# Moving the down products of a feed-forward pair one slot later, behind the first quarter of the next up chunk

## What is computed

```python
h = x @ w_in                       # columns q | k | v | u, 512 each
a_out = stick_breaking(q, k, v)    # 8 heads of 64, strictly causal
p_out = pool_mix(u)                # trailing means over 2, 4, 8, 16 tokens
x1 = LayerNorm(ALPHA * x + concat[a_out, p_out] @ w_out)
ffn = (silu(x1 @ w_gate) * (x1 @ w_up)) @ w_down        # hidden width 2816
y = LayerNorm(ALPHA * x1 + ffn)
```

## Time and profile before

| | before |
|---|---|
| median of three runs | 2588.72 us |
| span of the profiled execution, first to last instruction | 2585.7 us |
| PE busy | 2521.1 us, 98% of the span |
| VectorE busy | 1574.1 us, 61% |
| ScalarE busy | 1154.3 us, 45% |
| GpSimd busy | 1172.3 us, 45% |
| DMA | 374.43 MB, mean 145 GB/s |

### The profile page before, as it was taken

One profiled execution on the slowest core, in us unless ns is written; L12 is line 12 of the kernel. 1 busy time (PEld: TensorE's weight loads), 2 busy tenths in 40 slices (PEclk: granted clock), 3 DMA queues, 4 the chain that ended last, 5 costly groups with the idle time before them and its releaser, 6 DMA issues.

```text
span 2585.7 us, 37584 instructions
## 1 busy us (share of the span) xinstructions
PE 2521.1 (98%) x13894; PEld 2147.9 (83%) x13894; DVE 1574.1 (61%) x2125; ACT 1154.3 (45%) x1932; POOL 1172.3 (45%) x1028
## 2 busy tenths in 40 slices
PE   9999999999999999999999999999999999999998
PEld 9978798787878888878788877878878897999997
DVE  3266336666444357787744477787775345867676
ACT  4465326665232135566531265656654213343333
POOL 4465437755223135456631174556653213354434
PEclk9999999999999999999999999999999999999999
DMA  7697956764446243444254244333532612333232
GB/s 231 193 281 249 355 169 194 225 216 125 136 134 236 82 115 106 127 118 112 89 207 139 98 117 124 103 110 103 147 103 96 223 60 90 96 98 114 91 94 88
DMA packets 211158, 374.43 MB, mean 145 GB/s; under 512 B 30784, under 2 KB 105152, under 8 KB 208928
## 3 DMA queue, kind: packets, MB, share of 16 engines
q1 hardware_dynamic: 210976, 372.02, 45.7%
HBM read 303.86 MB, written 68.09 MB: 144 GB/s over the span
## 4 chain that ended last, share of the span: by engine, by line
PE 82%; DVE 7%; issue 4%; ACT 3%; POOL 2%; DMA 2%; SPq 1%; DVEq 0%; POOLq 0%; ACTq 0%
PE bank L1290 26%; PE bank L1352 19%; PE bank L1240 8%; PE bank L1194 7%; PE bank L1298 7%; PE bank L1092 5%; PE bank L1139 4%; PE bank L1108 4%; DVE left L1922 1%; DMA gw_lo_raw<-in_w_in_dram 1%; DVE acc L1960 1%; POOL gw_lo L2592 1%; PE bank L1217 1%; ACT beta L1476 1%; DVE stats L1942 0%
## 5 line engine op out<-in xcount | busy, mean ns | idle before, releaser
L1290 PE MATMUL bank<-x1T,gw_hi 128*128 128x512 f32 (+1 forms) x2336 | 712.2, 388 | 3.7 <-DVE hT_lo_raw L2036 2.3
L2522 POOL TENSOR_TENSOR beta<-beta,left 128x512 f32<-128x512 f32 (+2 forms) x326 | 352.5, 1082 | 349.7 <-DVE left L1922 349.2
L1290 PEld LDWEIGHTS bank<-x1T,gw_hi 128*128 128x128 f32 x2336 | 418.8, 188 | 83.7 <-issue 3.2
L1290 PE MATMUL bank<-x1T,gw_lo 128*128 128x512 f32 (+1 forms) x1168 | 447.9, 383 | 0.0
L2549 POOL TENSOR_TENSOR gw_lo<-gw_lo_raw,gw_hi 128x1024 fp32r<-128x1024 f32 x70 | 181.7, 2596 | 424.1 <-ACT gw_hi L1544 423.9
L1467 ACT ACTIVATE aT<-bank 128x512 fp32r<-128x512 f32 (+2 forms) x326 | 173.6, 533 | 427.4 <-PE bank L1108 376.0
L1240 PE MATMUL bank<-x1T,gw_hi 128*128 128x256 f32 (+2 forms) x1472 | 354.6, 333 | 6.3 <-DVE gw_lo L2231 2.5
L2217 DVE TENSOR_TENSOR acc<-bank,acc 128x512 f32<-128x512 f32 x312 | 213.3, 686 | 214.1 <-PE bank L1352 210.6
L1907 DVE TENSOR_TENSOR aT<-bank,aT 128x512 fp32r<-128x512 f32 (+2 forms) x326 | 196.9, 604 | 197.6 <-ACT aT L1467 196.3
L1352 PE MATMUL bank<-dw_hi,hT_hi 128*128 128x512 f32 x728 | 295.6, 406 | 9.8 <-issue 5.7
L1352 PE MATMUL bank<-dw_lo,hT_hi 128*128 128x512 f32 x728 | 287.0, 394 | 0.0
(11 more groups left out here) (223 smaller groups left out, 4709.3 us busy)
## 6 DMA issues: line engine op xcount, KB each, us to landing
gw_lo_raw<-in_w_gate_dram SPq DMA_DIRECT2D x88, 512.0 KB, 3.7
gw_lo_raw<-in_w_up_dram SPq DMA_DIRECT2D x88, 512.0 KB, 3.8
dw_lo_raw<-in_w_down_dram SPq DMA_DIRECT2D x86, 512.0 KB, 4.4
gw_lo_raw<-in_w_in_dram SPq DMA_DIRECT2D x64, 512.0 KB, 4.5
k_st<-kT_scratch SPq DMA_DIRECT2D x160, 128.0 KB, 4.1
v_st<-v_scratch SPq DMA_DIRECT2D x80, 256.0 KB, 4.2
q_st<-qT_scratch SPq DMA_DIRECT2D x128, 128.0 KB, 3.9
wo_raw<-in_w_out_dram SPq DMA_DIRECT2D x16, 1024.0 KB, 5.7
```

Of the source, the lines that this page charges most:

```text
L1290: m = pe.matmul(gu_bank(g, n)[:, 0:w], gw[L % 4][a][:, k, :], x1T[x][:, k, first:first + w], start=k == 0 and s == 0, stop=k == KD - 1 and ...
L2522: pool.tensor_tensor(x[:, 0:w], x[:, 0:w], left[n % RL][:, 1:w + 1], ALU.mult).then_inc(a_done, 1)
```

## The change

On every engine the block of eight slots that holds the down products of the pair before is moved behind the first slot of the up product of chunk 0. The slots of a pair are then: 0 to 3 gate of chunk 0, 4 the first quarter of up of chunk 0, 5 to 12 the down products, 13 to 15 the other three quarters of up, and 16 to 23 as before. The table `due` is not changed, so the attention and MIX steps keep their slot numbers. `sigmoid` of chunk 0 goes from slot 12 to slot 13, `times_gate` of chunk 0 from slot 13 to slot 14, and the load of the next `w_down` chunks from ahead of slot 12 to ahead of slot 13. In the first pair of blocks 1 to 3, where no down products stand, `sigmoid`, `times_gate` and the load move one slot later too. All else keeps its slot, among it the statistics and centring of the second layer norm in group 1, i = 2 (slot 14), which stand ahead of `times_gate` in the source.

```diff
+    STORE_PAIR, WINO_SHIFT, DOWNS_FROM = 4, 3, 1
...
@@ TensorE
-                    if p:
-                        for d in range(2 * tiles_of(b)):
-                            if not is_last(b, p):
-                                downs(b, p - 1, d)
-                            background(next(slot))
                     for e, g in ((0, 1), (1, 0), (1, 1)) if b + p else ((1, 0), (1, 1)):
                         for i in range(4):
+                            if (e, g, i) == (0, 1, DOWNS_FROM) and p:
+                                for d in range(2 * tiles_of(b)):
+                                    downs(b, p - 1, d)
+                                    background(next(slot))
                             gate(b, p, e, g, i)
                             background(next(slot))
...
@@ ScalarE
                     for i in range(4):
+                        if i == DOWNS_FROM and p:
+                            for d in range(2 * tiles_of(b)):
+                                background(next(slot))
+                                if before_wino and d in (2, 3, 4):
+                                    tokens_hi((3, 2, 4)[d - 2])
                         background(next(slot))
-                        if i == (0 if pair else 2):
+                        if i == (DOWNS_FROM if pair else 2):
                             sigmoid(b, p, 0)
...
@@ VectorE
                     for i in range(4):
+                        if i == DOWNS_FROM and p:
+                            for d in range(2 * tiles_of(b)):
+                                add_down(b, p - 1, d)
+                                background(next(slot))
...
                         now = ahead(next(slot))
                         second_norm(b, p, 1, i)
-                        if i == (1 if pair else 3):
+                        if i == (DOWNS_FROM + 1 if pair else 3):
                             times_gate(b, p, 0)
                         behind(now)
                         if i == 2 and before_wino:
                             tokens_lo(4, 2)
-                        if i != 1 and before_wino:
-                            quarter_sums(0, ((S_1, None, S_2, S_4)[i],))
+                        if i and before_wino:
+                            quarter_sums(0, ((None, S_1, S_2, S_4)[i],))
...
@@ SyncE (GpSimd's loop is moved in the same way)
-                    if p:
-                        for d in range(2 * tiles_of(b)):
-                            background(next(slot))
                     for i in range(4):
-                        if i == 0:
+                        if i == DOWNS_FROM and p:
+                            for d in range(2 * tiles_of(b)):
+                                background(next(slot))
+                        if i == DOWNS_FROM:
                             load_down(b, p)
                         background(next(slot))
```

More of the change, by code:

```diff
@@ L664, in stream @@
     SHIFT_AT = [(3, 0, 2), (3, 1, 0), (3, 2, 0), (4, 0, 2)]
-    STORE_PAIR, WINO_SHIFT = 4, 3
+    STORE_PAIR, WINO_SHIFT, DOWNS_FROM = 4, 3, 1
     with nc.Block() as block:
@@ L1812, in _ @@
                         second_norm(b, p, 0, i)
[L1813 to L1817, removed]
-                    for i in range(4):
+                    for i in range(4):
+                        if i == DOWNS_FROM and p:
[3 more added lines that the diff above has]
+                                    tokens_hi((3, 2, 4)[d - 2])
                         background(next(slot))
-                        if i == (0 if pair else 2):
+                        if i == (DOWNS_FROM if pair else 2):
                             sigmoid(b, p, 0)
@@ L2393, in _ @@
                         second_norm(b, p, 0, i)
[L2394 to L2402, removed]
-                    for i in range(4):
+                    for i in range(4):
+                        if i == DOWNS_FROM and p:
+                            for d in range(2 * tiles_of(b)):
+                                add_down(b, p - 1, d)
+                                background(next(slot))
+                                if before_wino and d in (0, 5, 8):
+                                    if d == 0:
+                                        token_sum(7)
+                                    else:
+                                        tokens_lo((3, 2)[d // 8], d // 8)
                         now = ahead(next(slot))
                         second_norm(b, p, 1, i)
-                        if i == (1 if pair else 3):
+                        if i == (DOWNS_FROM + 1 if pair else 3):
                             times_gate(b, p, 0)
```

## The result

| | before | changed |
|---|---|---|
| median | 2588.91 us (21 runs) | 2593.58 us (21 runs) |
| ratio, 95% interval | | 1.0018, 1.0013 to 1.0024 |
| span of the profiled execution | 2585.7 us | 2593.4 us |

The change costs 4.7 us by the medians (6.5 us were forecast), which is 0.18%, and 7.7 us between the two profiled executions. The two differ because of which executions were profiled. In the changed kernel's, the time (2595.22 us) is 1.8 us more than the span and 1.6 us above the median. So the 3.0 us that stood between span and median of before are not all outside the span.

What follows compares the result with a forecast made beforehand. The prediction took PE, busy 98% of the span, as the bound. Losses of 12.4 us plus 3.4 us of slow clock minus gains of 9.3 us made 6.5 us, so 2595.2 us; likeliest range 2593 to 2598, 8-in-10 range 2589.5 to 2600.

Steps and rivals of the forecast that it cites:

- gain at `hidden_lo`: PE's short waits ahead of the down products vanish with a slot more slack; 4.8 us gained.
- gain at `add_down`, pair 1.4: PE's wait at the down products for a late VectorE vanishes; 0.9 us gained with the overlap.
- pair 0.9, wait and clock: PE's wait for `add_down` goes, 1.9 us, and the slow clock behind it, 1.7 us.
- (a): Attention in slots 13 and 14 delays `times_gate` in pairs 1.2, 0.10, 1.9 and 2.5; 4.0 us lost.
- (b): Layer norm ahead of `times_gate` makes it late in pairs 2.0, 1.0, 1.1, 0.8 and 1.8; 5.8 us lost.
- (c): Chains from the later last down product, pairs 3.1 and 2.10, plus a subtraction in 2.8; 2.6 us lost.
- (d): Longer idle stretches in pair 2.10 and at 3.2 each bring slow clock, 1.7 us apiece; 3.4 us lost.
- Rival 2: A third of the 9.8 us `times_gate` losses returns in later waits, one clock drop comes; 2590.2 us, chance 0.13.
- Rival 1: The clock stays up or falls once more at most, rest as forecast; 2591.8 up to 2593.5 us, chance 0.24.
- Rival 3: `times_gate` is not late, so its losses and the clock drops fall away; 2582.0 us, chance 0.06.
- Rival 4: New waits for `summed` like pair 0.9's arise, each up to 1.9 + 1.7 us; 2600 us, chance 0.15.
- signs named ahead: PE's waits: "issue" under 2 us, `times_gate` about 11, six pairs over 1 each, line 1298 3.5, up weights about 3.

Runs made afterwards that it cites:

- e1: Changed kernel with sigmoid and `times_gate` of chunk 0 back where they stood before, so only the down products are later; 2587.06 us, 0.9997 of before.
- e2: Kernel before with only sigmoid and `times_gate` of chunk 0 one slot later, down products not moved; 2595.29 us, 1.0028 of before.
- e5: As e1, but with pairs 0.8, 1.8, 2.9, 2.10 and 3.1 entirely in the order of before; 2581.30 us, 0.9972 of before.
- e6: Changed kernel with `times_gate` of chunk 0 first in slot 14, ahead of that slot's attention and layer norm; 2586.35 us, 0.9990 of before.
- e8: Kernel before with only `hidden_lo` of chunk 1 moved ahead of VectorE's attention step of slot 2; 2582.93 us, 0.9981 of before.
- e4: Changed kernel with the edits of e1 and e3 together; 2587.49 us, 0.9997 of before.
- e9: e8 with down products one slot later in pairs 0.9 and 1.4 only, `times_gate` first in its slot there; 2580.66 us, 0.9968 of before.
- e10: e7 with e8's edit, `hidden_lo` of chunk 1 ahead of the attention step of slot 2; 2578.35 us, 0.9956 of before.
- e7: e6 with pairs 0.8, 1.8, 2.10 and 3.1 entirely in the order of before; 2582.01 us, 0.9973 of before.
- e3: Changed kernel with the old order in pairs 2.10 and 3.1 only; 2589.99 us, 1.0004 of before.
- e11: Changed kernel with GpSimd's two down-weight casts of pair 3.1 held back until VectorE's last cast for pair 3.2; 2592.52 us, 1.0017 of before.

## Why the prediction came out right

**The direction and most terms.** Forecast was a loss of 6.5 us; the ledger says 6.3, the medians 4.7. The time of 2593.58 us lies 1.6 us under the likeliest 2595.2 and in its range. The outcome by class was not the one that had the largest chance: +0.18% is "within 0.2%" (0.39), not "slower by over 0.2%" (0.55).

| step | forecast | ledger |
|---|---|---|
| gain at `hidden_lo` (0.1, 1.3, 1.10, 2.2, 2.5, 2.6) | -4.8 | -4.8 |
| gain at `add_down`, pair 1.4 | -0.9 | -1.07 |
| pair 0.9, wait and clock | -3.6 | -2.66 |
| (a) 1.2, 0.10, 1.9, 2.5 | +4.0 | +3.3 |
| (b) 2.0, 1.0, 1.1, 0.8, 1.8 | +5.8 | +5.8 |
| (c) 3.1 to 3.2, 2.10, 2.8 | +2.6 | +2.8 |
| (d) two stretches at 1.2 GHz | +3.4 | +2.4 |
| near 2543 us, not forecast | 0 | +0.6 |

(Pair 2.5's -0.73 is split by e1 and e2 into a gain of 0.9 and a loss of 0.2. How the clock is split off stands under "Sizes".) That the two sums agree to 0.2 us is in part luck: the losses (a) and (d) were taken 0.7 and 1.0 us too large, which the gain of pair 0.9, taken 0.9 too large, and the 0.6 us not foreseen nearly make up for.

**`times_gate` is the loss, the down products the gain.** e1 and e2 do the two halves of the change apart: -1.6 us and +6.7 us by the medians, together near the +4.7 of both. By the runs alone e1 is no faster than before (0.9988 to 1.0006); the gain of the later down products is seen in its ledger, where the six waits for `hidden_lo` and the two for `add_down` bring 8.6 us (1.6 of them the slow clock of pair 0.9), and in e5, which takes the losing pairs out and is 7.2 us faster. e6 shows that what makes `times_gate` late is what stands ahead of it in slot 14, as (a) and (b) had it, except in pairs 0.8 and 1.8.

**Waits for `hidden_lo`.** That PE waits because `hidden_lo` stands behind an attention step is shown by e8, which cures the waits by that order alone. The part of pair 2.6 that I took back (0.7) is right too: the changed kernel waits 0.80 us for the scan there, and e8, without that wait, gains 1.35 against 0.61.

**Sizes that were off.** In pair 0.9 I took the wait of 1.79 us for gained entirely. The changed kernel's timeline shows why it isn't:

```profile
968.71 0.41 PE L1108 MATMUL bank<-begin,beta 128*128 128x128 f32 x2 [0.47 <-POOL beta L2521]
```

PE, no longer held up by `add_down`, comes to its transposes before GpSimd's `beta` is there. In pair 1.9 the wait came (0.90 us idle), but PE's 0.36 us of "issue" five slots behind vanished with it, so 0.55 us stays of 1.2. In pair 0.8 the eighth down product waits 1.64 us and `times_gate` another 0.85, 2.4 us for my 1.8. In pair 2.8 `times_gate` stands behind both subtractions of line 1975, 6.68 us together where the second had taken 3.90 us before, 1.27 us for my 0.4. At pair 3.2 I carried the chain over as it was, 1.5 us longer. It got 0.8 longer, since one of VectorE's subtractions in it (`xt_lo`, line 2104 before, 2103 now) fell nearer to the end of the GpSimd cast beside it and took 2.80 us for 3.48 (below).

The slow clock (d) cost less than 1.7 us a stretch. In pair 2.10, e6 has the changed kernel's wait (2.80 us) and no slow stretch, and loses 0.76 us against 2.29, so the stretch cost 1.5 us. At pair 3.2 it cost up to 1.5 us by the 20th matmul behind the wait, but only 0.8 to 0.9 us from the 40th on, in each of the seven kernels that had it there (the changed one, e1, e4, e6, e8, e9, e10). Before, PE had waited another 0.42 us there for VectorE's `xt_lo`; a slower PE comes later and doesn't wait. The 0.6 us near 2543 us are a wait for VectorE (line 2113), with 1.2 us in e5, 0.6 in e4 and nothing in e7. Its cause is open.

**Rival 2, partly given back,** is refuted for the feed-forward pairs by e2's ledger: five losses of 0.55 to 1.38 us, and no pair behind them gains more than 0.03 us (0.9 apart, told above). Only the wait ahead of pair 3.2 is 0.7 us shorter there, 1.29 us, with `times_gate` in another place of VectorE's chain. The 3.0 us between the profiles' 7.7 and the medians' 4.7 are no time given back either. In the profiled executions the changed kernel had two more stretches at 1.2 GHz than the kernel before from 560 us on, 3.4 us. Averaged over the runs the clocks differ by 0.0008 (0.9973 in 31 runs of before, 0.9965), 2.1 us. That is 1.3 of the 3.0 us; the rest I can't place, and it is within what the stage ahead of pair 0.1 moves from one execution to the next (-1.5 to +3.4 us against before in these profiles).

**Rival 1, the clock,** did not come in the profiled execution, where the clock fell behind both waits. Behind the same two waits it stayed up in other kernels, so it was right to give it a chance: see below. **Rival 3** is refuted: PE waits 0.85 to 1.44 us for `times_gate` in every pair of (a) and (b) but 1.1 and 2.5, which had been put at 0.5 and 0.2 us. **Rival 4** did not come: the waits for `add_down` sum up to 3.3 us for 3.1 before, and the two long ones (1.64 us in pair 0.8, 1.24 in pair 2.10) stand where (b) and (c) had put something. Of the signs named ahead, "issue" (0.8 us), the waits for `times_gate` (9.8 for 11) and the up weights (2.8 for 3) came as said. Pairs 0.8 and 1.9 stayed under 1 us (0.85 and 0.90), and line 1298 waited 2.8 us for 3.5.

## What to carry to other kernels

When a consumer waits for a producer that stands behind other work on its engine, move the producer ahead of that work first: two lines on one engine (e8) brought 5.5 us and cost nothing elsewhere. A slot's shift of the down products on five engines cost 4.7 us, and brought 7.2 us only when the pairs were picked (e5). A slot of slack given to one dependency is taken from the others in the same ring, and before moving a block one lists the deadlines behind it, pair by pair, since the pairs that gain (idle ahead of the block) and those that lose (no slack behind it) are different ones and can be ordered differently. A ledger of the critical engine's progress between fixed marks tells what a wait is finally worth; sums of waits don't.

## What the runs showed of the hardware that I had not expected

**The length of an idle stretch of PE alone doesn't tell whether the clock falls.** In the feed-forward part of the 14 profiles PE had 71 idle stretches of over 1.2 us. A stretch at 1.2 GHz began in or behind 6 of the 46 under 1.7 us, 8 of the 15 up to 2.1 us, and 8 of the 10 longer ones. The place counts as well: all 6 of the short ones are the same wait in pair 0.4, near 757 us, where the clock fell in 6 of 8 cases, and it fell behind none of the 38 other stretches under 1.7 us. What sets that place apart isn't shown. The same stretch of 2.0 us ahead of pair 3.2 was followed by it in four kernels (e4, e8, e9, e10) and not in four others (before, e3, e5, e7), and 2.80 us in pair 2.10 went without it in e1 and e6. The wait in e1, and the window behind it:

```profile
2159.47 0.50 PE L1290 MATMUL bank<-x1T,gw_hi 128*128 128x512 f32 x1 [2.80 <-POOL gw_lo L2550]
```

```profile
2159.47:2162.88 3.41, 3.41 (x15) 2.77 (x16) 0.00 (x0) 0.00 (x0) 3.41 (x2) 1.00 0.02 8
```

Each time it lasted 3.41 us or twice that, and cost 0.8 to 1.6 us per 3.41 where the ledger can tell. A wait of this length is better priced with a chance than with a yes or no.

**VectorE beside GpSimd: one waits for the other.** In e11 and the changed kernel, instructions of VectorE with two inputs in SBUF took 1.5 to 2.2 us longer when they began while GpSimd was busy with a cast: 2.19 us for 0.68, 3.20 for 1.23, 2.34 for 0.18. Those that read a bank of PSUM did not (0.78 us for the two of `times_gate` in either case), nor did line 2081's, 1.75 us for 1536 columns, which had begun 0.46 us before the cast. The Trainium skill (GPSIMD Engine Reference, Specifications) says that GpSimd's SBUF interfaces are shared with VectorE, with contention where VectorE's instruction has two SBUF inputs. The traces agree, and they show its form. The 128x32 instruction paid 2.2 us, so the addition doesn't go by VectorE's size. It goes by what is left of GpSimd's instruction. In the 14 profiles 1261 instructions of VectorE with two inputs in SBUF began with over 0.3 us of a GpSimd instruction to go. 1233 of them took the time that the same shape takes alone plus that rest, less 0.08 to 0.19 us. The other 28, at two places of each profile, kept their own time, and there it was GpSimd's instruction, begun 0.4 us earlier, that took 2.58 us for 1.09. Of 7388 instructions that read PSUM and began in the same way, none was longer by over 0.15 us. So VectorE doesn't run slower beside GpSimd: it stands until GpSimd's instruction is nearly done, and the price of a meeting is what GpSimd has left. That is why the chain ahead of pair 3.2 came out 0.7 us shorter than carried over, and why holding the casts back (e11) only moved the cost to the next instructions.
